# Pieces of the output projection inside the last steps of the window attention, a thinner spread of one gate chunk, and modulation copies first in an mLSTM step

## What is computed

```python
for i in range(4):                      # mixers: window, latent, mLSTM, window
    sh, sc, gt = split(silu(c) @ w_ada + b_ada, 3)      # modulation of each layer, its weights are 6 blocks of 2 MB
    h = rmsnorm(x, g_pre) * (1 + sc) + sh
    y = mixer(h)
    x = x + gt * rmsnorm(y, g_post)     # layer 3: the 256 latent tokens alone

def window_mixer(h):                    # 16 heads of 64, 4 key heads
    q, k, v, z = split(h @ w_in)
    p = sink_softmax(mask(rope(q) @ rope(k).T * scale), sink)   # latent rows see 512 keys, context rows 256
    return ((p @ v) * silu(z)) @ w_out  # 1024 x 1024
```

## Time and profile before

| | |
|---|---|
| median of 3 runs (lowest, highest) | 1738.09 us (1732.26, 1743.22) |
| the profiled execution | 1736.09 us |
| its span in the trace | 1734.3 us |
| TensorE busy / weight loads / VectorE / ScalarE / GpSimd | 97% / 57% / 32% / 24% / 18% |
| mean granted TensorE clock | 0.994 |

### The profile page before, as it was taken

One profiled execution on the slowest core, in us unless ns is written; L12 is line 12 of the kernel. 1 busy time (PEld: TensorE's weight loads), 2 busy tenths in 40 slices (PEclk: granted clock), 3 DMA queues, 4 the chain that ended last, 5 costly groups with the idle time before them and its releaser, 6 DMA issues.

```text
span 1734.3 us, 18389 instructions
## 1 busy us (share of the span) xinstructions
PE 1681.6 (97%) x7081; PEld 982.3 (57%) x7081; DVE 561.9 (32%) x1602; ACT 413.4 (24%) x1070; POOL 304.8 (18%) x336
## 2 busy tenths in 40 slices
PE   5999998999999999999999999999999999999999
PEld 2455555454445544887465577644444544688854
DVE  2123433221334333565374423420142223232200
ACT  2003443120133221011153304510143331100000
POOL 0003544010000012431053104610212220000000
PEclk9999998999999999999999999999999999999999
DMA  9321321231251023122260432129452222344441
GB/s 396 134 97 49 146 97 50 97 120 38 94 198 49 25 99 145 54 93 97 98 243 25 176 117 87 60 94 190 184 193 104 92 97 101 143 152 162 165 152 49
DMA packets 17478, 206.47 MB, mean 119 GB/s; under 512 B 2056, under 2 KB 2584, under 8 KB 4976
## 3 DMA queue, kind: packets, MB, share of 16 engines
q1 hardware_dynamic: 15568, 195.74, 29.6%
q0 software_dynamic: 1824, 9.56, 2.7%
HBM read 201.08 MB, written 4.21 MB: 118 GB/s over the span
## 4 chain that ended last, share of the span: by engine, by line
PE 92%; DVE 3%; DMA 2%; POOL 2%; ACT 1%; issue 1%; SPq 0%; DVEq 0%; ACTq 0%
PE bank L661 41%; PE bank L1389 9%; PE bank L1128 7%; PE bank L740 5%; PE bank L754 5%; PE bank L1411 4%; PE bank L902 3%; PE bank L1040 2%; PE bank L706 2%; DMA ring<-stream 2%; PE bank L1016 2%; PE bank L1026 2%; PE bank L674 1%; POOL arena L2634 1%; PE bank L921 1%; PE bank L717 1%
## 5 line engine op out<-in xcount | busy, mean ns | idle before, releaser
L661 PE MATMUL bank<-ring,arena 128*128 128x512 f32 (+2 forms) x1360 | 560.5, 570 | 3.5 <-DVE arena L2004 1.3
L661 PEld LDWEIGHTS bank<-ring,arena 128*128 128x128 f32 x1360 | 255.5, 190 | 283.9 <-issue 268.9
L2634 POOL TENSOR_SCALAR arena<-arena,stat 128x512 f32<-128x512 f32 (+1 forms) x96 | 128.3, 1349 | 275.7 <-DVE stat L1573 275.7
L1389 PE MATMUL bank<-arena,ring 128*128 128x256 f32 (+1 forms) x768 | 152.8, 362 | 0.0
L661 PE MATMUL bank<-arena,ring 128*128 128x512 f32 (+2 forms) x400 | 148.8, 524 | 0.8 <-DVE arena L1451 0.8
L1389 PEld LDWEIGHTS bank<-arena,ring 128*128 128x128 f32 x768 | 136.0, 190 | 17.0 <-issue 0.5
L661 PEld LDWEIGHTS bank<-arena,ring 128*128 128x128 f32 (+1 forms) x400 | 74.2, 186 | 65.1 <-issue 59.6
L754 PE MATMUL bank<-ring,arena 128*128 128x512 f32 x192 | 90.7, 609 | 1.8 <-ACT arena L2359 1.2
L740 PE MATMUL bank<-arena,ring 128*128 128x512 f32 (+1 forms) x256 | 90.9, 498 | 0.0
L2271 ACT ACTIVATE arena<-arena,stat 128x513 f32<-128x513 f32 (+1 forms) x96 | 61.8, 646 | 79.2 <-DVE stat L1565 79.1
L740 PEld LDWEIGHTS bank<-arena,ring 128*128 128x128 f32 x256 | 46.2, 189 | 45.3 <-issue 42.8
(11 more groups left out here) (314 smaller groups left out, 1918.6 us busy)
## 6 DMA issues: line engine op xcount, KB each, us to landing
ring<-stream SPq DMA_DIRECT2D x88, 2048.0 KB, 7.8
ring<-stream SPq DMA_DIRECT2D x4, 1024.0 KB, 5.1
rev_scratch<-arena POOLq DMA_DIRECT2D x1, 3072.0 KB, 35.7
masks_sb<-masks POOLq DMA_DIRECT2D x2, 1024.0 KB, 6.0
arena<-g_scratch POOLq DMA_DIRECT2D x1, 2048.0 KB, 9.7
arena<-rev_scratch POOLq DMA_DIRECT2D x1, 2048.0 KB, 17.8
ring<-stream SPq DMA_DIRECT2D x1, 1536.0 KB, 6.4
arena<-x SPq DMA_DIRECT2D x1, 1024.0 KB, 10.2
```

What stands on the lines that cost most here:

```text
L661: last = mm(dst, a, b, start=(k == 0), stop=(k == len(pairs) - 1))
L1389: last = mm(ps[:, SEQ * part + cols.start:SEQ * part + cols.stop], w[:, a:a + P], hT2[:, k, cols], start=(k == 0), stop=(k == DC - 1))
L2634: nc.gpsimd.tensor_scalar(row, row, stat[:, 3, s:s + 1], None, ALU.mult).then_inc(w_norm, 1)
```

## The change

- `BESIDE[0]`: gate chunk 6 takes 4 steps of 2 products in place of 2 steps of 4. Everything after it in layer 0 moves two steps later.
- `FIRST_OUTPUTS` and `first_outputs`: the groups of tiles 0 and 1 of the output projection's first half are made in pieces inside the attention. In layer 0 tile 0 in steps 30 to 32 (3, 3, 2 products), tile 1 in steps 33 and 34 (4, 4); in layer 3 tile 0 in steps 14, 15 and 18 (3, 3, 2), tile 1 in steps 16 and 17 (3, 3), its last 2 products after the attention. Products go in the order in which quads finish and wait for `w_saved` of their quad.
- The two groups join `BESIDE_GROUPS`, so the banks of later groups turn by two places. In layer 0 tiles 2 and 3 then lie in banks 2 and 3. In layer 3 tile 0 of the second half takes bank 1 right behind tile 0 of the first.
- mLSTM on VectorE: `beside_step(2, i)` stands before `products(i)` and `reciprocals(i)`.

```diff
 BESIDE = {0: [("z", 1, 4), ("z", 2, 2), ("z", 3, 4), ("ada", 0, 8), ("ada", 1, 8), ("z", 4, 4), ("z", 5, 4),
-              ("z", 6, 4), ("z", 7, 4), ("ada", 2, 8), ("ada", 3, 8)],
+              ("z", 6, 2), ("z", 7, 4), ("ada", 2, 8), ("ada", 3, 8)],
...
+FIRST_OUTPUTS = {0: {30: (0, 0, 3), 31: (0, 3, 6), 32: (0, 6, 8), 33: (1, 0, 4), 34: (1, 4, 8)},
+                 3: {14: (0, 0, 3), 15: (0, 3, 6), 16: (1, 0, 3), 17: (1, 3, 6), 18: (0, 6, 8)}}
...
-BESIDE_GROUPS += STAGES["2 oT"][:6] + STAGES["2 y0"][:2]
+BESIDE_GROUPS += STAGES["2 oT"][:6] + STAGES["0 y0"][:2] + STAGES["2 y0"][:2] + STAGES["3 y0"][:2]
...
+                if layer in FIRST_OUTPUTS and i in FIRST_OUTPUTS[layer]:
+                    first_outputs(layer, *FIRST_OUTPUTS[layer][i])
+
+            def first_outputs(layer, t, a, b):
+                g, tiles = y_groups(layer)[t], LT if layer == 3 else TILES
+                if a == 0:
+                    begin(g)
+                w = weights(f"{layer} out0")
+                for slot in range(a, b):
+                    pe.wait_ge(w_saved, first_pair[layer] // 2 + slot // 2 * tiles + t + 1)
+                    k = Z_CHUNKS[slot]
+                    last = mm(bank[BANK_OF[g]][:, :], qT[:, slot, rows(t)], w[:, k * HALF:(k + 1) * HALF],
+                              start=(slot == 0), stop=(slot == DC - 1))
+                if b == DC:
+                    last.then_inc(made, 1)
...
+                        if KINDS[layer] == "window" and half == 0 and t < 2:
+                            done = max(b for g, _, b in FIRST_OUTPUTS[layer].values() if g == t)
+                            if done < DC:
+                                first_outputs(layer, t, done, DC)
+                        else:
+                            project(groups[half * tiles + t],
+                                    [(src[:, chunk(k), rows(t)], w[:, k * HALF:(k + 1) * HALF]) for k in range(DC)])
...
                 for i in range(n + 5):
+                    beside_step(2, i)
                     if i < n:
                         products(i)
                         reciprocals(i)
-                    beside_step(2, i)
```

More of the change, by code:

```diff
@@ L1167, in output_projection @@
                             pe.wait_ge(w_saved, (first_pair[layer] + len(window[layer])) // 2)
-                        project(groups[half * tiles + t],
-                                [(src[:, chunk(k), rows(t)], w[:, k * HALF:(k + 1) * HALF]) for k in range(DC)])
+                        if KINDS[layer] == "window" and half == 0 and t < 2:
[5 more added lines that the diff above has]
+                                    [(src[:, chunk(k), rows(t)], w[:, k * HALF:(k + 1) * HALF]) for k in range(DC)])
                         if half and t:
```

## The result

The changed kernel took 1720.14 us (median of 4 runs, 1719.79 to 1721.5), the kernel before beside it 1739.08 us (4 runs, 1732.26 to 1743.22). The ratio is 0.9896, 95% interval 0.9864 to 0.9929: faster by 1.04%, and within the interval by 0.7 to 1.4%. That it is faster is clear; whether it is so by more than the 1% that the prediction drew as its line is not. The forecast was 1721.5 us. The profiled execution took 1719.98 us with a span of 1718.2 us; before it was 1736.09 and 1734.3, so 16.1 us less, where the sum of the prediction said 16.6. The medians are 18.9 us apart, with an interval of 12 to 24 us, so only the traces can test the sum to a microsecond.

What follows compares the result with a forecast made beforehand. TensorE, busy for 97% of the span, was taken as the bound, with time lost in its waits and half clock. Gains of 9.2 (layer 0), 5.3 (layer 3) and 2.1 (mLSTM) sum to 16.6 us: 1738.09 to 1721.5 us, range 1714 to 1731.

Steps and rivals of the forecast that it cites:

- The bound: Whole kernel: TensorE is busy for 97% of the span; time comes off only where it waits or runs at half clock.
- Layer 0: Step 18 to the end of the projection's first half: 87.8 us after 97.0, gain 9.2 (5.1 clock, 4.1 waits).
- The lower bound of 3.0 us: Layer 0's smallest gain, if no clock comes back; the upper bound was 12 us.
- first rival: Whole kernel: half rate follows the many turns and stays; only waits go, 8.5 us, giving 1729.6 us; chance 0.20.
- Layer 3: Step 14 to the end of the second half: 40.5 us after 45.8, gain 5.3, with an added wait of 0.6.
- mLSTM: Earlier row copy on VectorE cuts TensorE's wait from 1.83 to about 1.0 us: gain 2.1 (0.8 wait, 1.3 clock).
- The banks: Groups behind the change: rotation by two keeps distances, but for a few that wait for groups saved microseconds before; no gain counted.
- Steps 2 to 13 as a proof of the clock: Layer 0: these steps ran at 1.00 with 3.0 us of waits, so the same steps in the tail would too.
- The chances: Whole kernel: 0.41 for over 1% faster (1720.7 us), 0.56 for within 1%, 0.03 for over 1% slower.
- The second (half clock falls on the moved products): Layers 0 and 3: moved products run at half rate, costing up to 25.8 us, 1755 us in all; chance 0.04.
- The third (more gain than forecast): All three places: remaining waits vanish too, up to 4.6 us more, 1717 us; chance 0.12.
- The fourth (pieces ahead of turns bring the waits back): Layer 0 gives nothing, layer 3 gives 3.6 and the mLSTM 0.8 us: 1733.7 us; chance 0.04.

Runs made afterwards that it cites:

- e6_fill: Kernel before plus five products nobody reads, one each in steps 28, 30, 32, 33 and 34 of layer 0: 1735.98 us, ratio 0.9985.
- e1_layer0: Kernel before with only layer 0's part: chunk 6 in four steps, five projection pieces, two groups in banks 0 and 1; 1730.8 us, ratio 0.9955.
- e8_split: Changed kernel with tile 0's last product moved from step 18 of layer 3 to behind the last outputs: 1720.51 us, ratio 0.9876 to the kernel before.
- e9_scores: Changed kernel with the scores of mLSTM unit 3 made in step 2, ahead of unit 0's turn: 1720.01 us, ratio 0.988 to the kernel before.
- e4_mlstm: Kernel before with only VectorE's order in the mLSTM changed, `beside_step` ahead of products and reciprocals: 1736.8 us, ratio 0.9998.
- e5_no_spread: Changed kernel with chunk 6 again in two steps of 4 products, steps 28 and 29 bare: 1726.93 us, ratio 0.9933 to the kernel before.
- e11_after_again: Changed kernel measured and traced once more without an edit: 1722.26 us, ratio 0.9897 to the kernel before.
- e7_late_copy: Changed kernel with VectorE's modulation copies in layer 0 behind the row maxima and reciprocals of their step: 1719.29 us, ratio 0.9887 to the kernel before.
- e3_banks: Kernel before with only the rotation of later groups by two banks, all products where they were: 1738.56 us, ratio 1.0001.
- e10_all: Changed kernel with the edits of e7_late_copy, e8_split and e9_scores together: 1715.47 us, ratio 0.9858 to the kernel before.

## Why the prediction was right, point by point

**The bound.** Right: time came off only where TensorE waited or ran at half clock, and the stretches between (545.74 and 191.77 us) are equal to 0.01 us. `e6_fill` shows the two together: filling the waits, even with work for nobody, brought the clock back.

**Layer 0.** Forecast 87.8 us, measured 87.67; gain 9.3 for 9.2. The split holds as well: waits from 7.1 to 3.0, so 4.1, and 5.2 for the clock. By parts it is 52.45 us for steps 18 to 29 (forecast 52.4), 21.29 for steps 30 to 34 (21.6) and 13.93 for tiles 2 and 3 (13.8), so two small errors cancel. The kernels that have the pieces and the spread and no other edit in layer 0 read 87.67 and 87.66 (the changed kernel twice), 87.67 (`e1_layer0`), 87.65 (`e8_split`) and 87.66 (`e9_scores`). It was foreseeable to a tenth because the changed tail repeats steps that the trace of before already held. The gain was not foreseeable so closely: the old tail took 95.81 to 98.57 us in four traces, and that the 96.97 of the first lies near their mean is luck. The lower bound of 3.0 us doesn't fit the prediction's own split either; with no clock back it is the 4.1 of its first rival.

**Layer 3.** Forecast 40.5, measured 40.35; gain 5.4 for 5.3. The added wait was 0.83 and not 0.6. What was mis-sized is the way back from VectorE. Its timeline in the changed kernel:

```profile
1132.99 0.42 DVE L1604 TENSOR_TENSOR arena<-bank,arena 128x256 f32<-128x256 f32 x1 [6.84 <-PE bank L1061]
```

It ends at 1133.41 and TensorE goes on at 1133.78: 0.37 us for the way back, where the forecast's 0.6 left 0.07 after 0.11 and 0.42. The rest of the stretch was 0.4 us shorter than summed.

**mLSTM.** Forecast 2.1, as 0.8 of waits and 1.3 of clock. The first was 1.0 (`e4_mlstm`): the wait behind was 1.20 and the row's turn came at once. Where no half clock stands in between, the turn of unit 0 starts 7.54 us behind the first scores in the old order (`e1_layer0`) and 6.78 in the new, which is the 0.8 of the forecast; the other 0.2 comes at the two turns of a later step, where the sum put nothing. The second is the step that fell: "if the shorter wait spares the half clock". The order on VectorE doesn't decide it. With the wait at 1.20 us half clock stood in the mLSTM in `e4_mlstm`, `e5_no_spread`, `e8_split` and `e11_after_again`, and was missing in the changed kernel's first trace and in `e7_late_copy`. With the old wait of 1.83 us it stood in four of five traces and was missing in `e1_layer0`. Where it is missing, 1.65 us go and not 1.3.

**The banks.** "Gives every later group the same distance ... which wait for groups saved microseconds before" was wrong in one place: a group of the last block had waited 0.53 us for its bank. A wait for a bank can sit far behind the change, where two rotations meet; `e3_banks` puts it at 0.6 us.

**Steps 2 to 13 as a proof of the clock.** The prediction took their 1.00 as evidence that the same steps in the tail would run at 1.00. They did in the tail. But in the changed kernel steps 2 to 13 themselves read 0.97, and half clock stands between 187 and 198 us in nine of the thirteen traces of this study, and of two traces of the one changed kernel it is 3.4 us long in one and 6.8 in the other. One trace of the clock is one draw. It cost 3.3 us in the first profiled execution (2.2 at the start, 1.1 in these steps), and 3.1 came back elsewhere (1.65 in the mLSTM, 1.45 behind the cumulated sum). The sum of 16.6 met the 16.1 of the traces partly because these cancelled. What belongs to the change and is backed by a kernel of its own is 9.3 + 5.4 + 1.0 + 0.6 = 16.3 us against the first trace of the kernel before; with the spread of its tail, 15 to 18 us.

**The chances.** The prediction gave 0.41 to faster by more than its 1% line and 0.56 to within it. The measured 1.04% sits on the line, so it speaks for neither.

**The rivals.** The first (the clock follows the turns) is refuted for layer 0 by `e6_fill` and by the tails of the changed kernel, and for layer 3 by the count: half clock in all five traces of the old tail, in none of the eight of the new, with the same turns. The second (half clock falls on the moved products) did not occur in any trace. The rule of the Trainium skill weighed for it, TensorE: Matmul & The Clock Gate, section "A second HAM failure mode: psum-queue depth-cycling", would have small idle times between groups in changing banks swing the clock. Here products, turns and outputs change banks in every step from 280 to 302 us and the clock is 1.00 with TensorE busy throughout; it is 0.79 and 0.66 in the kernel before, where the same turns have waits. So the changing banks alone do not bring it about, and the idle times may. The third (more gain than forecast) needed waits gone that all recurred: 3.0 us in layer 0, 0.83 in layer 3, 1.20 in the mLSTM. `e10_all` shows that they could be cut, by 2.8 us. The fourth (pieces ahead of turns bring the waits back) did not occur: no wait from step 30 on.

## What to carry to other kernels

On an engine that is 97% busy, look for the few places where it waits in a row, and move ready work there from a place where it has none to wait for; price the wait and the half clock that follows it together, since in layer 0 the clock was worth more than the waits (5.2 us for 4.1). Price such a stretch by a part of the trace that already has its shape, and only what is new by single rows. Then look at the first instruction behind the moved work: the cover it gave is gone there, and leaving one product behind (0.9 us) was enough to hide a wait of 0.8. Don't build on the clock of a single trace: compare stretches over several, of the kernel before as well, and count what repeats.

## What the runs showed of the chip

The granted clock is not fixed by the program. The same program started its first scores at 143.64 us in one trace and at 141.35 in another. In the first the second modulation product of the start ran long, 3.64 us for 16 records:

```profile
26.68 3.64 PE L711 MATMUL bank<-ring,cond_strip 128*32 128x512 f32 x16
```

and in the second it took 1.92:

```profile
26.03 1.92 PE L711 MATMUL bank<-ring,cond_strip 128*32 128x512 f32 x16 [0.45 <-DMA ring<-stream]
```

Nearly twice the time for the same product points to half the clock (1.2 in place of 2.4 GHz), but the clock column (the seventh figure) of the window reads 1.00 in the first trace. `e8_split` settles it. It starts its scores as late (143.66 us), its product takes the same 3.64 us, and the same window there reads 0.59. Here are the two windows, the changed kernel's first:

```profile
24.00:32.00 8.00, 8.00 (x47) 4.12 (x40) 4.38 (x8) 0.00 (x0) 0.00 (x0) 1.00 1.02 434
```

```profile
24.00:32.00 8.00, 8.00 (x47) 4.19 (x40) 4.38 (x8) 0.00 (x0) 0.00 (x0) 0.59 1.01 430
```

At the start the durations are the better witness.

The Trainium skill, TensorE: Matmul & The Clock Gate, section "What's actually happening", says that how much runs at half rate at a kernel's start varies between runs of the same kernel. The two traces of the changed kernel agree, by 2.3 us, and the traces show the same in the middle of the kernel: 0, 1.1 or 2.3 us in steps 0 to 18, 0 or 1.65 us in the mLSTM, 0 or about 1.4 us behind the cumulated sum. The single times of the kernel before spread from 1732 to 1743 us. That this comes from the clock is argued and not shown, since only profiled executions show their stretches.

Half clock followed short waits. The longest single wait of TensorE in layer 0 was 1.5 us in the tail of the kernel before and 1.6 in steps 2 to 13 of the changed one, and half clock stood behind both. But the kernel before had the same 1.6 us in steps 2 to 13 and 1.00 there, and so had the changed kernel in its tail: such a wait can bring half clock and need not. What a group of waits under 2 us cost in clock was the largest single term of this case (5.2 of 16.3 us).
